# GpSimd's weight splits behind VectorE's chains, block attention spread, half a projection tile among the score steps

## What is computed

```python
# first block, twice
z = rms_norm(x) @ w_in                         # latents, uv, pool input
a  = mla_mixer(...)                            # 4 heads, causal softmax attention
gm = sgu_mixer(uv); po = pool_mixer(pin)       # u * (w_spatial @ v);  window means
x = x + concat(rms_norm(a), rms_norm(gm), rms_norm(po)) @ w_out
x = x + (silu(h @ w_gate) * (h @ w_up)) @ w_down
# second block, twice
z = rmsnorm(x) @ w_in
y_hg, y_gla = chunked gated linear attention   # 4 + 4 heads
y_nsa = nsa_attention(...)                     # 8 heads: compressed keys (31 of them),
                                               # selected keys, a window of keys
m = g0*(y_hg @ w_br_hg) + g1*(y_gla @ w_br_gla) + g2*(y_nsa @ w_br_nsa)
x = x + m @ w_out;  then the same FFN
```

## Time and profile before

| | us |
|---|---|
| median of 3 runs | 3174.12 |
| lowest, highest | 3162.59, 3187.51 |
| the profiled execution, its own time | 3174.38 |
| its span in the trace | 3172.6 |
| TensorE busy | 3108.0 |
| VectorE busy | 1501.7 |
| ScalarE busy | 741.2 |
| GpSimd busy | 1903.6 |

### The profile page before, as it was taken

The page is one execution under the profiler, slowest core; times in us unless marked ns, Lnnn a source line. Parts: engine busy times, 40 slices in busy tenths (PEclk is TensorE's granted clock), DMA queues, the critical chain, the costliest instruction groups (busy, mean ns, idle before and its releaser), DMA issues.

```text
span 3172.6 us, 41836 instructions
## 1 busy us (share of the span) xinstructions
PE 3108.0 (98%) x15328; PEld 2497.0 (79%) x15328; DVE 1501.7 (47%) x2572; ACT 741.2 (23%) x1525; POOL 1903.6 (60%) x885
## 2 busy tenths in 40 slices
PE   8999999999999999999999999999999999999998
PEld 7688888868888888876688888888887668888887
DVE  4655421365541242886535455214388653545411
ACT  4410101341100222435601110012343560111000
POOL 4378778437787876001188777787600128877775
PEclk9999999999999999999999999999999999999999
DMA  3132333113232322111033332332211102332322
GB/s 122 49 107 97 99 93 100 67 40 107 93 99 94 105 82 85 48 47 61 18 96 97 96 99 93 99 100 87 87 48 48 60 21 94 100 99 94 99 93 86
DMA packets 71714, 262.31 MB, mean 83 GB/s; under 512 B 8208, under 2 KB 8208, under 8 KB 71440
## 3 DMA queue, kind: packets, MB, share of 16 engines
q1 hardware_dynamic: 71280, 258.34, 25.4%
q10 hardware_dynamic: 288, 1.98, 0.1%
HBM read 258.20 MB, written 2.10 MB: 82 GB/s over the span
## 4 chain that ended last, share of the span: by engine, by line
PE 88%; DVE 7%; issue 3%; ACT 2%; POOL 0%; DMA 0%; SPq 0%; DVEq 0%; ACTq 0%; POOLq 0%
PE bank L641 86%; DVE arena L1966 1%; PE bank L1268 1%; DVE h_lo L1990 1%; DVE rope L1966 1%; DVE rope L1963 0%; ACT arena L1903 0%; DVE arena L2507 0%; DVE bank L1966 0%; DVE arena L2335 0%; DVE arena L1963 0%; DVE arena L2523 0%; DVE w_lo L2361 0%; ACT arena L1889 0%; ACT act_hi L1547 0%
## 5 line engine op out<-in xcount | busy, mean ns | idle before, releaser
L1405 POOL TENSOR_TENSOR w_hi<-ring,one 128x1024 fp32r<-128x1024 f32 x430 | 817.7, 1902 | 1203.8 <-PE bank L641 1146.5
L1411 POOL TENSOR_TENSOR w_lo<-ring,w_hi 128x1024 fp32r<-128x1024 f32 x422 | 1040.7, 2466 | 33.1
L641 PE MATMUL bank<-h_hi,w_hi 128*128 128x512 f32 x2256 | 897.4, 398 | 4.6 <-DVE h_lo L1990 2.5
L641 PE MATMUL bank<-h_hi,w_lo 128*128 128x512 f32 x2256 | 882.5, 391 | 0.0
L641 PE MATMUL bank<-h_lo,w_hi 128*128 128x512 f32 x2256 | 881.5, 391 | 0.0
L641 PE MATMUL bank<-act_hi,w_hi 128*128 128x512 f32 (+1 forms) x1376 | 507.2, 395 | 8.0 <-issue 4.7
L641 PEld LDWEIGHTS bank<-h_hi,w_hi 128*128 128x128 f32 x2256 | 425.1, 188 | 99.2 <-issue 5.5
L641 PEld LDWEIGHTS bank<-h_hi,w_lo 128*128 128x128 f32 x2256 | 424.6, 188 | 91.7
L641 PEld LDWEIGHTS bank<-h_lo,w_hi 128*128 128x128 f32 x2256 | 425.3, 189 | 85.3 <-issue 1.0
L641 PE MATMUL bank<-act_hi,w_lo 128*128 (+1 forms) x1120 | 438.2, 391 | 0.0
L641 PE MATMUL bank<-act_lo,w_hi 128*128 (+1 forms) x1120 | 420.9, 390 | 1.4 <-DVE act_lo L2542 1.4
(11 more groups left out here) (245 smaller groups left out, 2921.2 us busy)
## 6 DMA issues: line engine op xcount, KB each, us to landing
ring<-wstream SPq DMA_DIRECT2D x480, 512.0 KB, 3.5
par<-params SPq DMA_DIRECT2D x4, 529.5 KB, 4.4
x<-xT SPq DMA_DIRECT2D x4, 512.0 KB, 7.5
outT<-h SPq DMA_DIRECT2D x4, 512.0 KB, 2.7
cst<-const ACTq DMA_DIRECT2D x1, 1412.0 KB, 8.8
par<-params ACTq DMA_DIRECT2D x1, 525.5 KB, 5.1
arena<-pos SPq DMA_DIRECT2D x1, 256.0 KB, 2.6
cst<-const SPq DMA_DIRECT2D x1, 24.5 KB, 2.4
```

The source lines that it names most:

```text
L641: return pe.matmul(out, lhsT, rhs, start=start, stop=stop)
L1405: return po.tensor_tensor(out, a, one.broadcast_to([P, n]), ALU.mult)
L1411: po.tensor_tensor(pair_[1], raw, pair_[0].bitcast(F32), ALU.subtract).then_inc(done.sem, 1)
```

## The change

1. **GpSimd waits longer** in five places. First mixer: split 9 also for both ropes (`hd_r(l, 2)`), split 11 also for VectorE's third squares (`mx_v(l, 3)`). Second mixer: merge split 0 for the compressed probabilities (`cs_p(l, 4)`), merge split 2 for VectorE's second rescale (`ns_c(l, 2)`). FFN: the second tile's low part for all eight `h_lo` (`f_ready(nf, ND)`).
2. **Block attention.** `pair_turn` takes the three groups of `TURNS`. ScalarE copies groups 0 and 1; VectorE copies group 2 (`last_turned`, signal `ns_od`), after the mask of step 4w+3. TensorE's order in a round becomes: score step, group 1 of w−2, score step, group 2 of w−2, values of 0 and 1, score step, values of 3, score step, values of 2, group 0 of w−1.
3. **First mixer.** The second half of `dense(17)` is put ahead of score steps 4 and 6, two blocks at each. ScalarE's copy of its result (`copy_z(17)`) follows the second exponential of window 1. The wait for `z_out` 18 moves behind the third turn. The pooled products are put ahead of and into `pv_pair(1)`. ScalarE's `out_square(2)` and `(3)` run ahead of the square root.
4. **Second mixer.** VectorE's `rope(6)` moves from ahead of `cmp_norm(0)` to behind `cmp_norm(1)`.

The core of the diff:

```diff
-        ns_t = later(at_t, 64)
-        ns_o = later(at_o, 64)
+        ns_t = later(at_t, 48)
+        ns_o = later(at_o, 32)
+        ns_od = later(lat_n, 16)
...
-                dense(17, 8)
+                dense(17, 8, range(4))
...
                         step = NT * w + t
+                        if step in (4, 6):
+                            dense(17, 8, (step, step + 1))
...
+                def pooled(b):
+                    pe.wait_ge(*pl_m(l, b + 1))
+                    if b:
+                        pe.wait_ge(*at_o(l, 12))
+                    product(pool_bank(b)[:, :], par[:, PAR1["w_pool"]][:, b * P:b * P + P],
+                            m1["win_m"][:, b, :]).then_inc(pl_mm.sem, 1)
...
                     for st in (0, 1, 3, 2):
+                        if w and st == 3:
+                            pooled(1)
...
                 score_pair(1)
-                pe.wait_ge(*z_out(l, 18))
+                pe.wait_ge(*z_out(l, 17))
                 turn_pair(0, 0)
...
                 turn_pair(0, 2)
+                pe.wait_ge(*z_out(l, 18))
                 pv_pair(0)
...
+                pooled(0)
                 pv_pair(1)
...
+                def pair_turn(w, g):
...
                     for e in range(2):
+                        if g > 0:
+                            pe.wait_ge(*ns_o(l, 4 * w + 2 * g + e - 1))
+                        elif w > 0:
+                            pe.wait_ge(*ns_od(l, 2 * w - 1 + e))
+                        for st in TURNS[g]:
+                            at = PT0[st] - TURN0[g][0]
...
                 for w in range(1, 9):
                     steps = steps_of(w)
+                    pair_scores(steps[0:1])
                     pair_turn(w - 2, 1)
-                    pair_scores(steps[0:1])
+                    pair_scores(steps[1:2])
                     pair_turn(w - 2, 2)
-                    pair_turn(w - 2, 3)
-                    pair_scores(steps[1:2])
...
                     pair_pv(w - 2, (0, 1))
-                    pair_scores(steps[2:4])
-                    pair_pv(w - 2, (2, 3))
+                    pair_scores(steps[2:3])
+                    pair_pv(w - 2, (3,))
+                    pair_scores(steps[3:4])
+                    pair_pv(w - 2, (2,))
                     pair_turn(w - 1, 0)
...
+                for g, part in enumerate(((0, 1, 2), (3, 4, 5), (6, 7))):
+                    if g > 0:
+                        pair_turn(7, g)
+                    merge_gate(1, EARLY + 1, part)
+                pair_pv(7, (0, 1, 3, 2))
...
                 times_one(pair_[0], raw, TILE).then_inc(high.sem, 1)
                 po.wait_ge(high.sem, count)
+                if clear is not None:
+                    po.wait_ge(*clear)
                 po.tensor_tensor(pair_[1], raw, pair_[0].bitcast(F32), ALU.subtract).then_inc(done.sem, 1)
...
                         po.wait_ge(*z_mm(l, (14, 17)[s - 8]))
+                        if s == 9:
+                            po.wait_ge(*hd_r(l, 2))
                     elif s in (10, 11):
                         po.wait_ge(*z_mm(l, 18 + s - 10))
+                        if s == 11:
+                            po.wait_ge(*mx_v(l, 3))
...
+                    if i == 0:
+                        po.wait_ge(*cs_p(l, 4))
+                    elif i == 2:
+                        po.wait_ge(*ns_c(l, 2))
...
+                               f_ready(nf, ND) if s == 1 else None)
...
-                copy_z(17, m1["u"][:, 0, :])
...
                 exp_pair(1, 1)
+                copy_z(17, m1["u"][:, 0, :])
...
+                for c in (2, 3):
+                    sc.wait_ge(*wo_r(l, c + 1))
+                    out_square(c)
                 sc.wait_ge(*mx_v(l, 4))
...
-                rope(6)
                 cmp_norm(0)
                 lows(14)
                 cmp_norm(1)
+                rope(6)
...
+                def last_turned(w):
+
+                    at, n = TURN0[2]
+                    if w:
+                        ve.wait_ge(*ns_v(l, w))
+                    for e in range(2):
+                        ve.wait_ge(*ns_t(l, 6 * w + 5 + e))
+                        ve.tensor_copy(nprobT[e][:, at:at + n], bank[6 + e][:, 0:n]).then_inc(ns_od.sem, 1)
...
                         last.then_inc(ns_m.sem, 1)
+                        if w >= 2 and step == NT * w + 3:
+                            last_turned(w - 2)
+                    if w == 8:
+                        last_turned(6)
+                last_turned(7)
```

More of the change, by code:

```diff
@@ L987, in mixer1 @@
                 turn_pair(1, 2)
-                for b in range(2):
-                    pe.wait_ge(*pl_m(l, b + 1))
-                    if b:
-                        pe.wait_ge(*at_o(l, 12))
-                    product(pool_bank(b)[:, :], par[:, PAR1["w_pool"]][:, b * P:b * P + P],
-                            m1["win_m"][:, b, :]).then_inc(pl_mm.sem, 1)
+                pooled(0)
                 pv_pair(1)
@@ L1254, in pair_scores @@
                         last.then_inc(ns_s.sem, 1)
-                def pair_turn(w, st):
+                def pair_turn(w, g):
                     if not 0 <= w < 8:
                         return
-                    if st == 0:
+                    if g == 0:
                         pe.wait_ge(*ns_c(l, w + 1))
                     for e in range(2):
-                        c = 8 * w + 2 * st + e
-                        if c >= 2:
-                            pe.wait_ge(*ns_o(l, c - 1))
-                        for t in range(st, NT):
-                            off = PS0[t] + st * P
-                            last = pe.transpose(bank[6 + e][:, (t - st) * P:(t - st + 1) * P],
-                                                nprob[w % 3][e][:, off:off + P], C("ident"))
+                        if g > 0:
[4 more added lines that the diff above has]
+                            at = PT0[st] - TURN0[g][0]
+                            for t in range(st, NT):
+                                off = PS0[t] + st * P
+                                last = pe.transpose(bank[6 + e][:, at + (t - st) * P:at + (t - st + 1) * P],
+                                                    nprob[w % 3][e][:, off:off + P], C("ident"))
                         last.then_inc(ns_t.sem, 1)
@@ L1287, in pair_pv @@
                                            nprobT[e][:, PT0[st]:PT0[st] + (NT - st) * P], win == 0 and st == 0, False)
-                    if win and NT - 1 in blocks:
+                    if win and 2 in blocks:
                         for e in range(2):
@@ L1294, in pair_pv @@
                                            m2["cmpT"][rows, hd // 4, :], False, True)
-                    if NT - 1 in blocks:
+                    if 2 in blocks:
                         last.then_inc(ns_v.sem, 1)
@@ L1308, in merge_gate @@
                         elif EARLY + 1 < n < EARLY + 4:
-                            pe.wait_ge(*ns_o(l, 64))
+                            pe.wait_ge(*ns_od(l, 16))
                         elif n >= EARLY + 4:
@@ L1405, in times_one, with halves @@
                 return po.tensor_tensor(out, a, one.broadcast_to([P, n]), ALU.mult)
-            def halves(raw, pair_, high, count, done):
+            def halves(raw, pair_, high, count, done, clear=None):
                 times_one(pair_[0], raw, TILE).then_inc(high.sem, 1)
                 po.wait_ge(high.sem, count)
+                if clear is not None:
+                    po.wait_ge(*clear)
                 po.tensor_tensor(pair_[1], raw, pair_[0].bitcast(F32), ALU.subtract).then_inc(done.sem, 1)
@@ L1486, in split @@
                     if s < FFN_TILES - 1:
-                        halves(raw, (w_hi[:, w, :], w_lo[:, w, :]), w_h, nf * w_h.per + it * 6 + (s + 1), w_split)
+                        halves(raw, (w_hi[:, w, :], w_lo[:, w, :]), w_h, nf * w_h.per + it * 6 + (s + 1), w_split,
+                               f_ready(nf, ND) if s == 1 else None)
                     else:
@@ L1679, in mixer1 @@
                 std(four(mx_std, 1), bank[6], 1 / 256, mx_sd)
-                for c in (2, 3):
-                    sc.wait_ge(*wo_r(l, c + 1))
-                    out_square(c)
                 for c in range(4, ND):
@@ L1899, in mixer2 @@
                             pair_out((w - 3) // 2)
-                        for st in range(NT):
+                        for g in range(2):
+                            at, n = TURN0[g]
                             for e in range(2):
-                                sc.wait_ge(*ns_t(l, 8 * (w - 1) + 2 * st + e + 1))
-                                sc.activation(nprobT[e][:, PT0[st]:PT0[st] + (NT - st) * P],
-                                              bank[6 + e][:, 0:(NT - st) * P], ACT.Copy).then_inc(ns_o.sem, 1)
+                                sc.wait_ge(*ns_t(l, 6 * (w - 1) + 2 * g + e + 1))
+                                sc.activation(nprobT[e][:, at:at + n], bank[6 + e][:, 0:n], ACT.Copy)\
```

(1 more changed line is left out.)

9 lines of the change are left out of this document (2 added, 7 removed).

## The result

| | before | after |
|---|---|---|
| median | 3174.41 | 3156.33 |
| lowest, highest of 13 runs each | 3162.59, 3187.51 | 3152.54, 3157.45 |
| span of the profiled execution | 3172.6 | 3152.7 |

The ratio is 0.9935, with a 95% interval of 0.9924 to 0.9946: faster, by 17 to 24 us; the medians differ by 18.1 and the spans by 19.9. That is inside the range on record, but 8 us over the forecast of 3148.

The account below looks back on a forecast made before the run. TensorE's chain was taken as the bound, busy 3108.0 of 3172.6 us. Terms −16 (attention), −3.1 (feed-forward starts), −2.5 (compressed keys), −1.4 (first mixer) and −3 (clock) sum to −26, giving 3148 us; range 3135 to 3167.

Parts of the forecast that it names:

- E: Block attention: VectorE locks step with TensorE, a round takes 10.9 us, +17 for −15, time 3181; chance 0.05.
- C: Block attention: ScalarE and its handshakes set the round at 8.7 us, −8 instead of −16, time 3156; chance 0.15.
- the first mixer: First mixer's reordering and holds: −0.7 us per layer, −1.4 in two layers.
- the attention's term: Second mixer's block attention: waits before transposes go, with the merge hold and tail; 8.1 us per layer, −16 in two.
- the clock: TensorE's half-clock pieces behind waits the change touches: two of eight taken as gone, −3 us.
- the small parts: Waits for h_lo at four feed-forward starts go, −3.1 us; rope(6) moved in the compressed keys, −2.5 us.
- two more switches: Block attention round: 0.2 us added for two more switches between products and transposes; new round 7.77 or 8.80 us.
- The collision: First mixer: GpSimd's eleventh split meets scale_pair(0)'s rescales, ending near 110.5; TensorE stands about 2.4 us, turn(0,0) 1.6 later.
- rival A: First mixer: the moved split misses scale_pair(0); −3.1 per layer instead of −0.7, time 3143; chance 0.15.
- the squares' order: First mixer: out_square(2) and (3) ahead of the Sqrt shorten TensorE's wait by 0 to 1.3 us; 0.8 taken.
- up to here −0.8: First mixer's scores: earlier start and dense(17)'s half filling the wait before 103.84 gain 0.8 us per layer.
- the wait of 1.40 before the pooled product at 128.89: First mixer: this wait goes with the lock on the 16-column product at 126.80, gaining 1.5 us per layer.

Follow-up runs that it names:

- the kernel with the small parts alone: Kernel before, plus only the second feed-forward tile's low part waiting for all h_lo and rope(6) behind cmp_norm(1); ratio 0.9957, median 3167.17.

## Why the prediction was right, and where it was off

**The direction, the range and the bound** held: TensorE's waits between the transposes, at the feed-forward starts and in the compressed keys went, and nothing but TensorE set the time in the attention's rounds. The rivals of a lock-step (E) and of ScalarE as the bound (C) fell to the chain after and to the kernel in which ScalarE does more. Yet C's number for the round, 8.7, is what was measured: the mean of 8.20 and 9.20. And C's time, 3156, is the measured median of 3156.33. Both right numbers stood at the wrong cause: ScalarE did not set the round, and C took its 8 us from the attention alone, which missed 3.2, while the first mixer missed 4.3.

Of the 8 us over the forecast the attention's term is 3.2 and the first mixer's 4.3; the clock and the small parts gave 2.7 more than forecast; the rest is the unassigned 0.7 of the table and the scatter of the medians around the profiled executions.

**The term of the attention was mis-sized**, −16 for −12.8. The step was "I add 0.2 us for two more switches", on 7.57 us of pure work. In the changed order nearly every piece changes its kind. Against the earlier trace rows: the three groups of transposes take 1.02 + 1.02 + 0.59 = 2.63 and not 2.35, and the 28 products 1.06 + 3.66 = 4.72 and not 4.37. That is 0.63 in place of 0.2. The first 0.28 of it is a misreading: eight transposes were put at 0.93 us, the row's 1.09 less 0.16, but the next product starts 1.02 after them, so the row overlaps it by 0.07 only. Some of what was called a wait in the old round was the transposes' own time. The tail and the holds made up part of it: the holds gave 1.2 and not 0.5.

**The clock's term** had the right sign, −3 for −5.1, but "two gone" was a choice and not a sum: in sum three pieces went, and that it came so near is luck. The rule of the Trainium skill, "TensorE: Matmul & The Clock Gate", section "HAM oscillation — how this bites in real kernels", that idle time between bursts brings the clock down, is borne out at one place: behind the wait of 1.9 us before turn(0,0), the half-clock stretch is there in 9 of 10 layers of the five kernels with that wait, and in none of the six layers of the three kernels that have the new order of score steps without the wait. It doesn't account for the 10.2 us at 643.70, which came without such a wait; that stretch stands once in each of the four kernels with the old order of score steps, in the first layer or the second, and in none of the eight with the projection tile spread among them. So the spreading may be what removes it, worth 5.1 us, which is more than the first mixer loses below. The kernel with the first mixer as before has the stretch again, but it undoes more than the spreading, so this is not shown. What brings the stretch on in one layer and not the other is open. The last piece that the prediction named, at 2476.60, stayed (2465.0 in the changed kernel): it stands ahead of the wait that rope(6) made, not behind it.

**The first mixer** is where the forecast had the wrong sign: −1.4 for +2.9, its clock left out. Two of its steps were right. The collision came where it was worked out and nearly as large (rescales until 109.38 and not 110.5, TensorE's wait 1.9 and not 2.4), so that rival A fell; and the squares' order gave 1.1 by itself, where 0.8 stood. A third, "up to here −0.8", was off: by the nth products it is −0.2. Six products set between score steps take 1.59 us in the changed kernel (98.46 to 100.05), not 6 × 0.226 = 1.36, since the kind changes on both sides, and that happens twice. With the smaller collision it nearly cancelled, by luck: turn(0,0) comes 1.8 us later for the forecast 1.6.

The step that failed is "and with it the wait of 1.40 before the pooled product at 128.89", booked as a gain of 1.5 that nothing takes back. The wait went, but the product's results were not followed further. The second pooled product feeds ScalarE's square and copy, VectorE's sum of squares and then TensorE's token sums; put into the value products it made ScalarE stand 3.36 us for it, and a wait of 1.90 (2.06 with the 0.16) appeared before those sums, beside the 0.49 at 130.17. The wait before the output part became shorter for it, 0.70 for 2.37. The rule was at hand: for a moved step, name who waits for its result. The half-clock stretch behind the collision was not in the sum either; it cost 1.7 us.

**The small parts** were right within 0.3 us: −3.4 for −3.1 and −2.8 for −2.5, and each shows in the kernel with the small parts alone.

The Trainium skill, "SBUF — State Buffer", section "Who interferes with whom", says that whoever issues first holds the shared pair for its whole instruction; by that rule the moved split lands on what comes next. The trace agrees: 6.18 us for rescales that take 2.46.

## What to carry to other kernels

A hold placed on an engine's split doesn't remove the split: work out on whom it lands next, and hold it behind that one too. When waits are filled by interleaving, count a price for every change between kinds of matmul (0.08 to 0.17 us here), and interleave only where a wait is really there. Compare two long kernels by the start of the nth product and keep the half-clock stretches as a term of their own, since they can hide the sign of a part's effect.

## What was unexpected of the hardware

Changes between kinds of matmul cost time at full clock and with no wait shown. In the changed kernel's rounds a group of eight transposes takes 1.02 us and one of four 0.59, so four more take 0.43, and each group adds 0.16 for going to transposes and back, 0.08 a change. Going from score products to value products and back costs 0.35 for the pair, about 0.17 each. And half-clock stretches of 3.4, 6.8 or 10.2 us, between 27.3 and 51.2 us in all per profiled execution, stood at places that differ between kernels that are the same up to there: the sum of a few waits can be doubled or cancelled by them.
